# Expert rows of a mixture-of-experts layer: loaded in quarters and transposed by VectorE instead of TensorE

## The reference, cut to what matters

```python
u = rms_norm(x, norm2_g) * (1.0 + sc2) + sh2           # sc2, sh2, g2: one value per feature
aff = softmax(u @ w_router)                            # 16 experts
gate = ...                                             # best of 4 groups, top-2 experts in it, weights normed to 1
for e in range(16):
    h = silu(u @ w1[e]) * (u @ w3[e])                  # w1, w3: (1024, 512)
    y = y + gate[:, e:e + 1] * (h @ w2[e])             # w2: (512, 1024)
x = x + g2 * y
```

## Time and profile before

| | |
|---|---|
| median of 3 runs | 756.02 us (754.96 to 758.34) |
| the profiled execution, its own time | 755.66 us |
| its span | 754.0 us |
| first matmul of the expert stage | 428.19 us |
| end of its last matmul | 724.86 us |
| busy: TensorE, VectorE, ScalarE, GpSimd | 81%, 43%, 34%, 11% of the span |
| moved by DMA | 176.26 MB, mean 234 GB/s |

### The profile page before, as it was taken

How to read it: one execution, slowest core, us unless ns; L and a number is a source line. 1 busy time by engine, 2 the same in 40 slices (tenths; PEclk the granted TensorE clock), 3 DMA queues, 4 the chain that set the end, 5 groups by cost and what they waited for, 6 DMA issues and landing times.

```text
span 754.0 us, 15645 instructions
## 1 busy us (share of the span) xinstructions
PE 613.6 (81%) x6231; PEld 362.8 (48%) x6235; DVE 322.3 (43%) x925; ACT 255.4 (34%) x611; POOL 80.2 (11%) x119
## 2 busy tenths in 40 slices
PE   0798999977689988799981388999999999999940
PEld 0544474664356666555440254555555555555520
DVE  3713818233279999933336022232232232222215
ACT  3300200113356677822330143433443343344310
POOL 5001000016100000000002200101110110110022
PEclk9998999989779999999995599999999999999985
DMA  8970957061499300056019649999999999999228
GB/s 326 378 306 7 395 212 276 3 204 30 151 335 216 110 1 1 2 207 240 1 48 350 215 167 363 360 372 361 364 375 359 365 375 361 365 366 362 61 60 302
DMA packets 81389, 176.26 MB, mean 234 GB/s; under 512 B 9410, under 2 KB 26378, under 8 KB 79306
## 3 DMA queue, kind: packets, MB, share of 16 engines
q1 hardware_dynamic: 68592, 152.90, 57.9%
q0 software_dynamic: 8384, 13.97, 5.5%
q10 hardware_dynamic: 4380, 8.94, 3.8%
HBM read 155.02 MB, written 20.71 MB: 233 GB/s over the span
## 4 chain that ended last, share of the span: by engine, by line
PE 25%; DMA 24%; issue 3%; DVE 2%; POOL 2%; ACTq 0%; ACT 0%; POOLq 0%
DMA featT<-expert_rows 22%; PE score L1595 9%; PE score L1495 7%; PE bank L1585 4%; PE score L1604 3%; DMA pool_sb<-expert_rows,idx 1%; POOL pool_sb L805 1%; POOL expert_rows L785 1%; DMA expert_rows<-pool_sb,idx 1%; DMA expert_rows<-featT 1%; PE bank L1530 0%; PE bank L1610 0%; ACTq L680 0%; PE bank L1539 0%; PE bank L1550 0%
## 5 line engine op out<-in xcount | busy, mean ns | idle before, releaser
L1595 PE MATMUL score<-pool_sb,featT 128*32 128x256 f32 x2688 | 162.3, 386 | 20.8 <-DMA featT<-expert_rows 12.1
L1595 PEld LDWEIGHTS score<-pool_sb,featT 128*32 128x32 f32 x2688 | 86.7, 111 | 82.4 <-DMA featT<-expert_rows 26.8
L1291 PE MATMUL bank<-pool_sb,featT 128*128 128x512 f32 (+2 forms) x256 | 88.7, 509 | 5.8 <-DVE featT L860 2.6
L1231 DVE TENSOR_TENSOR featT<-featT,score 128x128 f32<-128x128 f32 x42 | 12.1, 288 | 184.7 <-ACT featT L691 184.7
L1604 PE MATMUL score<-pool_sb,featT 128*32 128x256 f32 x1344 | 82.3, 386 | 0.4 <-ACT featT L696 0.4
L1291 PEld LDWEIGHTS bank<-pool_sb,featT 128*128 128x128 f32 x256 | 49.9, 196 | 43.1 <-issue 35.4
L685 ACT ACTIVATE featT<-bank,mod_col 128x32 f32<-128x32 f32 x129 | 39.4, 375 | 61.2 <-PE bank L1585 61.2
L793 POOL DMA_DIRECT2D expert_rows<-featT x42 | 29.2, 695 | 277.8 <-DVE featT L1227 264.0
L1221 DVE TENSOR_SCALAR featT<-bank,mod_col 128x32 f32<-128x32 f32 x215 | 51.0, 304 | 14.9 <-PE bank L1585 14.9
L1495 PE MATMUL score<-pool_sb,featT 128*128 128x512 f32 x128 | 56.9, 597 | 0.0
L691 ACT ACT_TABLE_LOAD x42 | 53.9, 1283 | 0.8
(11 more groups left out here) (255 smaller groups left out, 679.6 us busy)
## 6 DMA issues: line engine op xcount, KB each, us to landing
pool_sb<-in_moe_w SPq DMA_DIRECT2D x48, 2048.0 KB, 22.2
pool_sb<-in_ada_w SPq DMA_DIRECT2D x16, 1024.0 KB, 7.3
expert_rows<-zeros_f SPq DMA_DIRECT2D x17, 512.0 KB, 6.5
featT<-expert_rows ACTq DMA_DIRECT2D x44, 128.0 KB, 5.4
expert_rows<-featT POOLq DMA_DIRECT2D x42, 128.0 KB, 7.0
pool_sb<-in_ada_w SPq DMA_DIRECT2D x8, 640.0 KB, 11.8
pool_sb<-in_w_out SPq DMA_DIRECT2D x4, 1024.0 KB, 16.7
pool_sb<-in_ada_w SPq DMA_DIRECT2D x8, 384.0 KB, 9.7
```

The costliest lines, as they stand in the source:

```text
L1291: m = nc.tensor.matmul(pj_bank(g, i)[:, 0:n], featT[:, k, i * P:(i + 1) * P], w_stage[:, g % 3, k, 0:n], start=(k == 0), stop=(k == KD - 1))
L1595: mm = nc.tensor.matmul(banks[0][h * BT:(h + 1) * BT, 0:2 * HB], xgT[:, k, :], exp_w13[slot][:, :, k, h * HB:(h + 1) * HB], start=(k == 0) ...
```

## The change

Three things change in the expert stage, and one ahead of it.

First, x_hat writes the columns of a row in another order: quarter h of the row holds, for each of the 8 pieces of 128 features, the 32 features that will lie on partitions 32h to 32h+31. Second, a block is loaded as 128 partitions (32h + r) by 256 columns, in 1 KB runs, into one of two buffers, and GpSimd asks for it, two blocks ahead. VectorE multiplies it by a scale and adds a shift, both laid out once in the same order, and then transposes it with one instruction in 32x32 squares, which gives `xgT` as before. In the same way `hmid` is transposed by VectorE: for that the columns of w1 and w3 are read in runs of 32. Third, TensorE is left with inner and outer only, and ScalarE with silu only. The load of the last matrix of expert 2 now waits for the scatter alone. The DMAs of the weights are the same lines in both versions.

```diff
-        xg = blkbuf[0:BT, 0:D]
+        xg = [blk_view(DN) for _ in range(2)]
+        xm = blk_view(DN)
...
-            sp.wait_ge(s_xg, 32)
+            sp.wait_ge(s_scat, 16 * 2 * TT)
             load_matrix(2, 0)
...
+                nc.scalar.activation(norm_x[:, i, :].rearrange("p (h j a) -> p j h a", h=NT, a=BT),
+                                     x_sb[:, i, :].rearrange("p (j h a) -> p j h a", h=NT, a=BT), ACT.Copy,
+                                     scale=rstd2[:, i:i + 1]).then_inc(r_xh, 1)
...
+            def xg_load(g, n):
+                pool.dma_start(xg[n], xs[bass.ds(g * BT, BT), :].rearrange("r (h n) -> h r n", h=NT)).then_inc(s_xg[n], 16)
+            pool.wait_ge(s_scat, 16 * 2 * TT)
+            for g in range(4):
+                if g >= 2:
+                    pool.wait_ge(m_sc, g - 1)
+                xg_load(g, g % 2)
             with pool.Fori(0, pairs - 1) as m:
                 for n in range(2):
+                    pool.wait_ge(m_sc, m * 2 + (n + 3))
+                    xg_load(m * 2 + (n + 4), n)
                     store_rows(y_sb[n], m * 2 + n, n)
...
+            for k0, to in ((16, scale2_part), (24, shift2_part)):
+                nc.vector.tensor_copy(xm.rearrange("p (k r) -> p k r", r=BT), mod_col[:, k0:k0 + KD].unsqueeze(2).broadcast_to([P, KD, BT])).then_inc(m_part, 1)
+                dve.wait_ge(m_part, k0 // 4 - 3)
+                nc.vector.transpose(to[:], xm).then_inc(m_part, 1)
+                dve.wait_ge(m_part, k0 // 4 - 2)
+            def rows_in(g, n):
+                dve.wait_ge(s_xg[n], g * 8 + (16 if n == 0 else 8))
+                if not (isinstance(g, int) and g == 0):
+                    dve.wait_ge(m_xT, g)
+                nc.vector.tensor_tensor(xm, xg[n], scale2_part[:], ALU.mult).then_inc(m_sc, 1)
+                dve.wait_ge(m_sc, g + 1)
+                nc.vector.tensor_tensor(xm, xm, shift2_part[:], ALU.add).then_inc(m_mod, 1)
+            def xg_T(g):
+                dve.wait_ge(m_mod, g + 1)
+                nc.vector.transpose(xgT.rearrange("p k r -> p (k r)"), xm).then_inc(m_xT, 1)
+            def hmid_T(g):
+                dve.wait_ge(m_h, g + 1)
+                nc.vector.transpose(hT.rearrange("p k r -> p (k r)"), hmid).then_inc(m_hT, 1)
+            def hidden(g):
+                dve.wait_ge(m_h1, g + 1)
+                xg_T(g + 1)
+                dve.wait_ge(m_si, g + 1)
+                nc.vector.tensor_tensor(hmid, silu, banks[0][:, HB:2 * HB], ALU.mult).then_inc(m_h, 1)
+            def block_of_rows(g, n, y):
+                hidden(g)
+                dve.wait_ge(m_y, g)
+                hmid_T(g)
+                rows_out(y)
+                rows_in(g + 2, n)
...
             def inner(slot, g):
+                pe.wait_ge(m_xT, g + 1)
                 for k in range(KD):
-                    if k == KD - 1:
-                        pe.wait_ge(s_xg, g * 16 + 32)
+                    w = exp_w13[slot][:, :, k, :].rearrange("p m (c h a) -> p m c h a", h=NT, a=BT)
                     for h in range(NT):
-                        mm = nc.tensor.matmul(banks[0][h * BT:(h + 1) * BT, 0:2 * HB], xgT[:, k, :], exp_w13[slot][:, :, k, h * HB:(h + 1) * HB],
+                        mm = nc.tensor.matmul(banks[0][h * BT:(h + 1) * BT, 0:2 * HB], xgT[:, k, :], w[:, :, :, h, :],
...
             def stage_of(g, slot, slot_before, uses):
                 pe.wait_ge(e_w13[slot], uses * 32)
+                pe.wait_ge(m_h, g)
                 inner(slot, g)
-                xg_T()
                 pe.wait_ge(e_w2[slot], uses * 16)
                 outer(g - 1, slot_before)
-                inner_T(g)
```

More of the change, by code:

```diff
@@ L180, in decoder_layer, with blk_view @@
         blkbuf = featT[:, :, :].rearrange("p k n -> p (k n)")
-        xg = blkbuf[0:BT, 0:D]
[L182 to L187, removed]
+        blk_at = [0]
+        def blk_view(n):
+            blk_at[0] += n
+            return blkbuf[:, blk_at[0] - n:blk_at[0]]
+        xg = [blk_view(DN) for _ in range(2)]
+        xm = blk_view(DN)
+        xgT = blk_view(DN).rearrange("p (k r) -> p k r", r=BT)
+        silu = blk_view(HB)
+        hmid = blk_view(HB)
+        hT = blk_view(HB).rearrange("p (k r) -> p k r", r=BT)
+        y_sb = [blk_view(DN) for _ in range(2)]
+        y_last = [blk_view(DN) for _ in range(2)]
         yab = ring[:, :, 0:TT * D].rearrange("p b (i n) -> p b i n", i=TT)
@@ L334, in decoder_layer @@
         s_scat = sem("s_scat")
-        s_xg = sem("s_xg")
+        s_xg = [sem(f"s_xg{n}") for n in range(2)]
+        m_mod = sem("m_mod")
+        m_sc = sem("m_sc")
+        m_part = sem("m_part")
         m_h1 = sem("m_h1")
@@ L1237, in _ @@
+            hidden(0)
+            hmid_T(0)
+            rows_in(2, 0)
             dve.wait_ge(t_gs, 1)
@@ L1239, in _ @@
             for g in range(1, 3):
-                block_of_rows(g)
-                rows_out(y_sb[(g - 1) % 2], g)
+                block_of_rows(g, g % 2, y_sb[(g - 1) % 2])
             with dve.Fori(1, pairs - 1) as m:
[L1243 to L1249, removed]
-            last = dve.value_load(block_start[0:1, NE + 2:NE + 3], min_val=MIN_BLOCKS * NE - 1, max_val=MAXB)
-            rows_out(y_last[0], last)
-            rows_out(y_last[1], last + 1)
+                for n in range(2):
+                    hidden(m * 2 + 1 + n)
+                    dve.wait_ge(m_y, m * 2 + 1 + n)
+                    hmid_T(m * 2 + 1 + n)
+                    dve.wait_ge(s_ys[n], m * 16)
+                    rows_out(y_sb[n])
+                    rows_in(m * 2 + 3 + n, 1 - n)
+            last = dve.value_load(block_start[0:1, NE + 2:NE + 3], min_val=MIN_BLOCKS * NE - 1, max_val=MAXB)
+            hidden(last)
+            dve.wait_ge(m_y, last)
+            hmid_T(last)
+            rows_out(y_last[0])
+            dve.wait_ge(m_y, last + 1)
+            rows_out(y_last[1])
             for i in range(TT):
@@ L1580, in _, with inner @@
             m.then_inc(r_rank, 1)
-            def xg_T():
+            def inner(slot, g):
+                pe.wait_ge(m_xT, g + 1)
                 for k in range(KD):
[L1584 to L1591, removed]
-                    if k == KD - 1:
-                        pe.wait_ge(s_xg, g * 16 + 32)
+                    w = exp_w13[slot][:, :, k, :].rearrange("p m (c h a) -> p m c h a", h=NT, a=BT)
                     for h in range(NT):
-                        mm = nc.tensor.matmul(banks[0][h * BT:(h + 1) * BT, 0:2 * HB], xgT[:, k, :], exp_w13[slot][:, :, k, h * HB:(h + 1) * HB],
+                        mm = nc.tensor.matmul(banks[0][h * BT:(h + 1) * BT, 0:2 * HB], xgT[:, k, :], w[:, :, :, h, :],
                                               start=(k == 0), stop=(k == KD - 1))
```

60 lines of the change are left out of this document (15 added, 45 removed).

## The result

The changed kernel takes 768.86 us (median of 4 runs, 766.73 to 770.15) against 757.18 (754.96 to 759.47): 1.5% slower, ratio 1.0151, interval 1.0109 to 1.0193. 741.6 was predicted, in a range of 736 to 750. The profiled execution took 768.24 us, its span is 765.9. TensorE's last outer ends at 737.26 instead of 724.86; what follows it is the same to half a microsecond.

What follows compares the result with a forecast made beforehand. Bound: the row-load loop, 6.9 us a block, leaving TensorE 15 us behind its weights, the next bound. Last outer 724.9 to 710.5 saves 14.4: 754.0 - 14.4 + 1.7 = 741.3, adjusted for the profiled run to 741.6; range 736 to 750.

Steps and rivals of the forecast that it cites:

- the price of the load's traffic: Row loads in 1 KB runs on GpSimd's queue: same traffic cost as before, within 1% of the stream, 2.5 us either way.
- the DMAs stay full and the stream keeps its rate: Weight loads from expert 5 on: five matrices stay outstanding, so the rate holds, 19.2 us an expert at 364 GB/s.
- B: Rival in the expert stage: rows stay late or the weight stream slows, 4% being 10 us; 751 us, chance 0.10.
- TensorE's block: Expert stage: without transposes, row waits and the load loop, a block takes 5.75 us instead of 6.9.
- the term of 0: Inner's moving operand in 8 runs of 32 columns adds 0 to the matmuls; the upper bound was twice the time.
- The allowance of 0.2 for the loop: Expert stage: average loop gap of about 0.2 us added to 5.52 us of TensorE work a block.
- VectorE: Expert stage: added transposes (0.43 and 0.29 us) and operations, 0.9 us beside outer and 1.9 beside inner, are covered.
- The start: First blocks: rows at 430.0, first inner at 431.5, 3.3 us later; stream 1 us late, bounds -2.5 and +3.
- the estimate of 2.3 us for the load: First row load alone, by the skill's fixed 2 us plus bytes; start up to 3 us sooner than with the 6.5 taken.
- TensorE meets the stream from expert 5: Expert stage: TensorE passes experts 1 to 4 by 502 us, then waits for most experts' w1 and w3, 2 to 8 us.
- Rival A, the clock: TensorE's clock goes cold at each weight wait, costing 4 to 6 us over experts 13 to 15; 747 us, chance 0.14.
- The rest of the sum: Whole kernel: 754.0 - 14.4 = 739.6 us span, plus 1.7 around it, 741.3; forecast 741.6 us.

Runs made afterwards that it cites:

- a5: The changed kernel with each block's row load, still asked for by GpSimd, split into four DMAs of 32 partitions of 1 KB; 741.01 us, ratio 0.9786.
- a1: The changed kernel with the row loads asked for by ScalarE's queue instead of GpSimd's, same 1 KB runs and buffers; 785.03 us, ratio 1.0374.
- a8: a1 with each block's rows loaded by two DMAs of outermost dimension 2; 840.88 us (one run).
- a4: a1 with each block's rows loaded by four DMAs of 32 partitions of 1 KB; 737.40 us, ratio 0.9739.
- a7: a1 with one load a block of outermost dimension 128, rows landing in another order, output not the reference's; 727.89 us (one run).
- b2: The kernel before with each block's row store split into four DMAs of 32 partitions; 749.75 us, ratio 0.9892.
- a6: a4 with stores also in four DMAs and expert 2's last matrix waiting for the first two row loads; 726.99 us, ratio 0.9602.
- b1: The kernel before with inner reading w1 and w3 in runs of 32 columns, output not the reference's; 758.62 us (one run).
- a2: The changed kernel with the load of expert 2's last matrix waiting for the first two row loads; 763.53 us, ratio 1.0083.
- a3: The changed kernel with GpSimd loading rows as 32 partitions of 4 KB into unread buffers, output not the reference's; 757.56 us (one run).

## Why the prediction was wrong, point by point

**The step that failed is "In 1 KB runs I take the same (bounds: 1% of the stream quicker, 1% slower, 2.5 us either way)", the price of the load's traffic, and with it "the DMAs stay full and the stream keeps its rate".** The DMAs stayed full (1.05), but the stream moved 343 GB/s instead of 366 and took 9% longer, 23.6 us. I priced the loads by bytes and share of engine time, and that share was even right: loads and stores took 12.7% of it, and 6.5 + 5.8 = 12.3% before. What I did not ask is which of the 16 engines do the work. The access pattern `"r (h n) -> h r n"` stands in the diff, and its outermost size is 4. With the quartered load cut in four, and nothing else changed, the rate is 371 GB/s and the time 741.0 us (a5).

The Trainium skill has the rule (DMA: Bandwidth & Descriptors, Why a DMA increments its semaphore by 16 and not by 1): a DMA runs on the largest number up to 16 that divides the outermost dimensions of both sides; those from SyncE and ScalarE use the lowest-numbered engines, those from GpSimd take the next ones in turn. The small packets on ScalarE's queue and the row packets under way at once agree with the number, 4, 2 and 16. That they are always the same engines on ScalarE's queue and others each time on GpSimd's fits a1 being worse than the changed kernel (785 and 769), but no view names an engine; that part is argued, not shown.

How the narrow form costs can be seen on ScalarE's queue only: a few engines are late with their part of the weights while the others stand idle (in a8 just one or two weight packets are under way for 23 of the 190 us). In the changed kernel itself the engines stood idle hardly more than before (16 or more packets under way 94% of the time, 96% before); there each weight packet of 4 KB took longer (195 ns for 175; 178 in a5). Why it does is open. The spread alone does not set it, for the kernel before, with its loads on 16 engines in 4 KB packets, moves 366 GB/s, and a4, on as many in 1 KB packets (and with quicker blocks), 379.

The rival was near: B had a slower stream, by 4% where 9% came, and as its cause the 1 KB runs, which a4 and a7 clear. Against it I wrote that the stores have the same shape and cost no more. They had the same shape, and b2 shows that they did cost there: 366 to 379 GB/s. A row that carries the fault itself was my evidence that there was none. What a quartered store costs hangs on the loads beside it, though: a7 keeps the stores as they were and moves 390 GB/s, a6 with its stores cut in four 388.

**TensorE's block: right, too careful.** 5.75 predicted, 5.18 measured. Inner stays at 3.66 with its 8 runs (the term of 0 holds, b1). The 58 ns of an outer matmul came from 1.86 us; the row shows 1.93, 60 ns, which changes nothing here. The allowance of 0.2 for the loop was not needed, and inner and outer overlap by 0.37 us in all (3.64 + 1.91 - 5.18) where I took 0.07.

**VectorE: right.** 0.45 and 0.31 us measured for the two transposes, 0.43 and 0.29 taken; twice the width does not take twice the time.

**The start: direction right, too small.** Rows at 432.2 (430.0 predicted), first inner at 433.7 (431.5), expert 3 asked for at 449.8 (447.5): 3.3 us late, just past the bound of 3. The cause named is the one that a2 shows; it is worth 5 us. Beside it the estimate of 2.3 us for the load would have put the start 4.2 us sooner than 6.5 does, not 3; without the collision a2 has 3.9 us.

**TensorE meets the stream from expert 5: right but for one expert.** It first waits ahead of the first block of expert 4, counted from 0 as in the prediction (timeline):

```profile
492.74 5.35 PE L1619 MATMUL score<-pool_sb,featT 128*32 128x256 f32 x64 [2.52 <-DMA pool_sb<-in_moe_w]
```

Missed there: before the outer of an expert's last block TensorE waits for w2 of the *next* expert, since `e_w2[slot]` stands ahead of it in stage_of. These are the 23.8 us in 11 waits at L1628. TensorE's lag had hidden it. At the end it costs the wait at 727.38, 2.25 us.

**Rival A, the clock:** it came, and cost little. The granted clock was 0.90 over the window, and an inner behind a wait of 2.1 us or more took 5.2 to 5.8 us in six of seven cases, 3.66 in the other. But expert 15 still waited for its weights (1.32 us at 721.46, 2.25 at 727.38), so what the low clock cost ahead of it does not reach the end. In a4 it is 0.92 and the time still 737.

**The rest of the sum stands to a few us:** a4, the changed kernel with wide loads from ScalarE, is at 737.4 and a5 at 741.0; 741.6 was forecast. That a5 hits it so closely is in part luck: its stream moved 371 GB/s where the sum has 364, by my estimate 5 us in its 250.

One question is open: a3's loads are wide (up to 16 packets under way, stores included), and still it moved 355 and not 366. It may be that GpSimd's queue costs something of its own (355 against the kernel before's 366, and a5's 371 against a4's 379), and that TensorE's quicker blocks crowd the stores; neither was tried alone. Between a3 and a5, both wide and both on GpSimd's queue, the row packets went from 4 KB to 2 KB and the rate from 355 to 371; the size of the packets was not tried alone either.

## What to carry to other kernels

Before a transfer's shape is changed, read the outermost size of both sides of its access pattern, not only bytes and run length: where that was 4, the transfer used 4 of 16 DMA engines, and the weights queued beside it came 9% later. Idle engines beside a full queue (a1, share 0.96), or a full share beside a falling rate (the changed kernel, 1.05 at 343 GB/s), is how it looked in the profile; the number of small packets for each DMA on ScalarE's queue told the width. And when a new operation is priced by an old one of the same shape, the old one may already be paying.

## What the runs showed of the hardware that was not expected

Row loads of 128 KB a block, 5% of the bytes, set the rate of all the rest: 281, 325, 379 GB/s with ScalarE's loads on 2, 4 and 16 engines (a8, a1, a4), and 390 GB/s with one load on 16 (a7, up to 680 us). The short packets did no harm here: with loads on 16 engines a4 moves 379 GB/s in 1 KB packets, the kernel before 366 in 4 KB packets. A 2 MB load that was queued in the same microsecond held back a row load of 128 KB from 3.9 (a2) to 8.6 us. VectorE transposes 128x256 float32 in 32x32 squares in 0.45 us, about as long as it takes to multiply it.
